# A product of the state-space tables moved behind the next pair of weight chunks, and a memory column moved between two groups of state inputs

## The chip, the core and the metric

The kernel runs on one core of a Trainium2 chip, as one program for the whole inference step. The metric is the device time of one execution in microseconds (us), the median of the runs. The core's engines are called PE (TensorE matmul; PEld is its weight load), DVE (VectorE), ACT (ScalarE), POOL (GpSimd) and SP (SyncE, which here only issues DMAs). Each engine works through its own list of instructions in order; semaphores tie the lists together.

## The reference, cut to what matters

The model is a two-layer decoder trunk on 512 prompt tokens and 8 sample tokens of width 1024, all in float32:

```python
for i in range(2):
    x = x + 0.5 * swiglu(rmsnorm(x), ffn1_w_in[i], ffn1_w_out[i])
    x = x + mixer[i](rmsnorm(x))          # layer 0: S5 state-space block, layer 1: HGRN2
    x = x + cross_attend(rmsnorm(x), mem_k[i], mem_v[i], w_q[i], w_o[i])
    x = x + 0.5 * swiglu(rmsnorm(x), ffn2_w_in[i], ffn2_w_out[i])
y = rmsnorm(x)
mem_k[i], mem_v[i] = split(rmsnorm(mem) @ xattn_w_kv[i])   # 256 memory tokens, 2048 columns
```

The S5 block drives 64 groups of 16 channels, each with a 64-dimensional complex diagonal state: state input B u, a scan over the tokens, output C h + d u. All of these are outputs: the trunk's result, the final states and the memory keys and values.

## The kernel before, in words

**Matmuls.** Every weight matrix is streamed as chunks of 128 columns, two chunks to a pair. A float32 chunk arrives in `raw`, ACT rounds it to a high part `w_hi` (line 1330), DVE subtracts to get a low part `w_lo` (lines 1827 and 1833), and PE multiplies high x high, high x low and low x high into the bank `lin` (lines 3019 and 3024). `ffn1_out0` of layer 0 has four pairs with 11 tiles to a chunk; behind it comes `ffn1_in1`, with 8 tiles to a chunk.

**The tables of the state-space block.** While the first feed-forward block runs, the S5 tables are made. POOL builds eight parts a = 0 to 7 in order; for each one it makes `sFe` and then `sGe` with twelve tensor operations (lines 736 to 738) and counts up `s5_tables` after each of the two (line 1191 for `sGe`). PE then has three groups per part: two transposes F (line 2560) and one product K (line 2567, then line 2570). K of part a waits in PE's list until `s5_tables` says that `sGe` of part a is there:

```python
pe.wait_ge(s5_tables, 2 * a + 2)
```

The function `hook` runs at the end of a pair, on PE, ACT and DVE alike, and calls `prepare(first, end)` for the range of groups that the dictionary `PREP` names for that pair. Before the change, pair a of `ffn1_out0` takes F, F and K of part a for a = 0 to 3; parts 4 to 7 follow in `ffn1_in1`, each after another two pairs. The eight groups in question use the `mis` banks in turn, four of them, and a group waits until ACT has emptied the bank of the fourth group before it. ACT copies F into `sTF` (line 1462) and K into `sKst` (line 1467). `sKst` is one buffer: the copy of part a waits until SP has written part a - 1 to memory (line 946, eight DMAs). SP does that in its own hook, `K_OUT`; for part 2 it comes behind the weight loads of the first pair of `ffn1_in1`, and the loads of the second pair are queued behind it. POOL may build `sGe` of part a only after PE's K of part a - 2.

**The state-space block.** Its order on PE, ACT and SP is the list `S5_ORDER`. PE transposes the normalised tokens (X, line 2717), transposes them again by chunk (U, line 2724) and multiplies them with the tables (FU, line 2732, 16 matmuls to a group). Groups FU 0 to 7 belong to the first half of the states, FU 8 to 15 to the second. DVE scans the first half while FU 8 to 15 run, and the second half after it. Then come the outputs Y and y.

**The memory columns.** Between these groups PE computes the 16 columns of memory keys and values of layer 0 (`kv_step`, matmuls on line 2512, 24 to a column; line 2523 turns the previous column inside the next one). Before the change columns 0, 1 and 2 stand behind FU 15. Column 0 waits for both halves of the normalised memory, `m_hi` and `m_lo`, 1 MB each, which SP loads (line 818) once FU 7 is done, since `m_hi` lies where the first half's tables lay:

```python
if c == 0:
    pe.wait_ge(mem_in[l], 32)
```

On ACT, `kv_step` empties the column (line 1414), splits the weights two columns ahead (line 1403) and copies the turned column out (line 1425).

Of the kernel before, what the change touches and what calls it, by code (L numbers as in the profile page):

```python
# [134 lines left out]
def trunk_kernel(nc, i_, o_):  # L135
# [137 lines left out]
    c = o_hid + 2 * FRONT + 4096  # L273
    pZ = at("pZ", [P, 2, MH, NS, NS], F32, c); c += 2048
    assert c <= o_hid + KD * FRONT
    c = o_lo + 2 * FRONT + 4096
# [9 lines left out]
    c = o_s0  # L286
# [20 lines left out]
    c = o_hid + (FH + KD) * HTILE  # L307
# [6 lines left out]
    c = o_zeros  # L314
# [9 lines left out]
    c = o_s0  # L324
# [18 lines left out]
    c = o_ah + NJ // 2 * (1 + UC) * 4  # L343
# [297 lines left out]
    PREP = {("ffn1_in0", 0, 0): (0, 4), ("ffn1_in0", 0, 2): (4, 9), ("ffn1_in0", 0, 3): (9, 10)}  # L641
    K_OUT = {}
    for a in range(8):
        PREP["ffn1_out0" if a < 4 else "ffn1_in1", 0, a if a < 4 else 2 * a - 7] = (len(made), len(made) + 3)
        K_OUT["ffn1_out0" if a < 2 else "ffn1_in1", 0, a + 2 if a < 2 else a - 2 if a < 4 else 2 * a - 5] = a
        made += [("F", 2 * a, "act"), ("F", 2 * a + 1, "act"), ("K", a, "act")]
    S5P = Groups(made, s5p_fill, s5p_void, banks=4)
    MEM_NORM = {("ffn1_in0", 0, 4 + v // 2, v % 2): v for v in range(3)}
    MEM_SPLIT = {("ffn1_in0", 0, 5 + (v + 1) // 2, (v + 1) % 2): (v // 4, KD // 4 * (v % 4)) for v in range(8)}
# [25 lines left out]
    KV_AFTER = {None: [0, 1, 2], 0: [3, 4], 1: [5, 6], 2: [7, 8], 3: [9, 10], 4: [11, 12], 5: [13], 6: [14], 7: []}  # L675
    HIDDEN = [(0, 0, 6, 1), (0, 6, 7, 1), (1, 0, 3, 1), (0, 7, 8, 1), (1, 3, 6, 2), (1, 6, 8, 2)]
    assert sum(part[3] for part in HIDDEN) == KD
    S5_ORDER = []
    for q, (what, a, _) in enumerate(made):
        S5_ORDER.append(("group", q))  # L680
        if q + 1 == S5G.after("FU"):
            S5_ORDER += [("kv", c) for c in KV_AFTER[None]]
        if what == "Y" and a[1] == 1:
            S5_ORDER += [("kv", c) for c in KV_AFTER[a[0]]]
    S5_ORDER.append(("kv", KV - 1))
# [55 lines left out]
    with block:  # L741
        @block.sync
        def _(sp):
# [179 lines left out]
            def hook(name, layer, i):  # L923
# [8 lines left out]
                if at_ in K_OUT:  # L932
                    a = K_OUT[at_]
                    sp.wait_ge(s5_tables, 2 * a + 2)
                    for e in range(2):
                        sp.dma_start(s5_g[4 * a:4 * a + 4, :, P * e:P * (e + 1)].rearrange("j p n -> p j n"),
                                     sGe[a % 2][:, e, :, 1:, :].rearrange("p j d c -> p j (d c)"))\
                            .then_inc(s5_g_out[a % 2], 16)
                    S5P.emptied_of(sp, "K", a)
                    row = SG * 256  # L940
# [76 lines left out]
        def _(pool):  # L1017
# [11 lines left out]
            pool.nop().then_inc(s5_small, 1)  # L1029
            S5P.all_emptied(pool, S5P.at("m", 3) + 1)  # L1030
            step.link(pool.tensor_tensor(m_acc[:], mT[:, 0, :], mT[:, 0, :], ALU.mult))
# [74 lines left out]
            def s5_discretize():  # L1106
# [3 lines left out]
                pool.wait_ge(mem_squares, 1)  # L1110
                S5P.emptied_of(pool, "par", 0)
                ar, ai, ld = par[:, 0:32], par[:, 32:64], par[:, 64:96]
# [54 lines left out]

                S5P.emptied_of(pool, "c", (1, 1))
                pool.wait_ge(s5p_fill, S5P.at("c", (1, 1)) + 1)
                pool.wait_ge(vec_done, 1)  # L1170
# [8 lines left out]
                for a in range(8):  # L1179
# [7 lines left out]
                    if a >= 2:  # L1187
                        pool.wait_ge(s5p_fill, S5P.at("K", a - 2) + 1)
                        pool.wait_ge(s5_g_out[a % 2], 16 * 2 * (a // 2))
# [1995 lines left out]
```

## Time and profile before

| what | value |
|---|---|
| runs shown | 2360.42, 2360.5 and 2362.08 us, median 2360.5 |
| the profiled execution | 2360.95 us, of which the span from first to last instruction is 2359.2 |
| mean granted clock of TensorE | 0.998 of full speed |
| busy share of the span | PE 99%, PEld 96%, DVE 55%, ACT 37%, POOL 26% |
| the chain that ended last | PE 91%, DVE 4%, POOL 2%, ACT 1%, issue 1%, DMA 1% |

The profile is of one execution. Times in it are microseconds from the first instruction. A busy PE leaves the other engines room; what counts are the few places where PE stands idle or runs at the lower clock.

### The profile page before, as it was taken

How to read it: one execution, taken by the hardware profiler on the slowest of the kernel's cores; microseconds unless marked ns; L12 is line 12 of the kernel's file. 1: busy time of each engine (PE TensorE's matmuls, PEld its weight loads, DVE VectorE, ACT ScalarE, POOL GpSimd, SP SyncE). 2: the span in 40 equal slices, each digit the busy share in tenths (PEclk: the TensorE clock that was granted, in tenths of full speed). 3: DMA queues.
4: the chain of work that ended last, by engine and by line, in shares of the span. 5: the costliest groups of instructions: out<-in, count | busy, mean ns of one | idle time of the engine just before them, and what ended most of it. 6: DMA issues, size and time to landing. Idle time of an engine off the chain costs nothing.

```text
span 2359.2 us, 50146 instructions
## 1 busy us (share of the span) xinstructions
PE 2335.6 (99%) x21043; PEld 2273.7 (96%) x21043; DVE 1295.1 (55%) x1906; ACT 869.1 (37%) x1399; POOL 605.4 (26%) x591
## 2 busy tenths in 40 slices
PE   9999999999999999999999999999999999999999
PEld 8999999889979999999999999999999979999999
DVE  6653643964576443445543344577777666443443
ACT  4432333453233321322433233267775233321323
POOL 3779967431103000004111010432122102000003
PEclk9999999999999999999999999999999999999999
DMA  5456445553563333333543333233332653333332
GB/s 160 130 160 153 122 136 165 175 171 107 161 245 86 98 99 89 98 96 98 159 118 111 100 108 115 83 100 107 104 108 77 214 188 91 97 94 94 98 94 94
DMA packets 483707, 289.19 MB, mean 123 GB/s; under 512 B 22289, under 2 KB 466962, under 8 KB 482514
## 3 DMA queue, kind: packets, MB, share of 16 engines
q1 hardware_dynamic: 477856, 280.66, 40.3%
q0 software_dynamic: 560, 1.84, 0.6%
q10 hardware_dynamic: 5122, 4.25, 0.5%
q8 instruction: 129, 2.11, 0.4%
q14 instruction: 40, 0.33, 0.0%
HBM read 258.86 MB, written 27.85 MB: 122 GB/s over the span
## 4 chain that ended last, share of the span: by engine, by line
PE 91%; DVE 4%; POOL 2%; ACT 1%; issue 1%; DMA 1%; SPq 0%; DVEq 0%; POOLq 0%; ACTq 0%
PE lin L3019 51%; PE lin L3024 25%; PE mis L2512 4%; PE mis L2650 1%; PE mis L2633 1%; POOL sTmp L737 1%; PE lin L2600 1%; PE lin L2762 1%; PE lin L2981 1%; PE lin L2757 1%; POOL sGe L738 0%; PE lin L2650 0%; DVE w_lo L1827 0%; PE mis L2626 0%; POOL sFe L738 0%
## 5 line engine op out<-in xcount | busy, mean ns | idle before, releaser
L1827 DVE TENSOR_TENSOR w_lo<-raw,w_hi 128x1024 fp32r<-128x1024 f32 (+1 forms) x322 | 463.8, 1440 | 294.4 <-ACT w_hi L1330 293.7
L1330 ACT ACTIVATE w_hi<-raw 128x1024 fp32r<-128x1024 f32 (+1 forms) x328 | 365.1, 1113 | 311.3 <-PE lin L3024 257.7
L3019 PE MATMUL lin<-a_rear,w_hi 128*128 128x264 f32 x3552 | 455.6, 279 | 0.0
L3019 PE MATMUL lin<-a_front,w_hi 128*128 128x256 f32 x3552 | 451.6, 279 | 1.1 <-DVE a_rear L1840 0.7
L3019 PEld LDWEIGHTS lin<-a_rear,w_hi 128*128 128x128 f32 x3552 | 432.7, 188 | 0.0
L3019 PEld LDWEIGHTS lin<-a_front,w_hi 128*128 128x128 f32 x3552 | 424.5, 188 | 4.6 <-issue 1.8
L3024 PE MATMUL lin<-a_rear,w_lo 128*128 128x264 f32 x1776 | 245.1, 278 | 0.0
L3024 PE MATMUL lin<-a_front,w_lo 128*128 128x256 f32 x1776 | 240.6, 277 | 0.9 <-DVE w_lo L1827 0.9
L2391 DVE SCALAR_TENSOR_TENSOR xT<-lin,xT 128x520 f32<-128x520 f32 (+1 forms) x87 | 60.8, 699 | 322.9 <-PE lin L3024 322.2
L1063 POOL TENSOR_TENSOR acc<-xT 128x520 f32<-128x520 f32 x8 | 12.2, 1520 | 864.0 <-DVE xT L2391 836.0
L3024 PEld LDWEIGHTS lin<-a_rear,w_lo 128*128 128x128 f32 x1776 | 223.8, 188 | 0.0
L3024 PEld LDWEIGHTS lin<-a_front,w_lo 128*128 128x128 f32 x1776 | 219.6, 188 | 1.6 <-DVE w_lo L1827 1.5
L1741 ACT ACTIVATE f_front<-t 128x256 fp32r<-128x256 f32 (+1 forms) x88 | 36.9, 419 | 398.3 <-DVE t L2372 398.3
L3019 PE MATMUL lin<-f_rear,w_hi 128*128 128x264 f32 x1386 | 179.9, 283 | 0.0
L3019 PEld LDWEIGHTS lin<-f_rear,w_hi 128*128 128x128 f32 x1386 | 172.1, 189 | 0.2
L3019 PE MATMUL lin<-f_front,w_hi 128*128 128x256 f32 x1386 | 170.3, 276 | 0.0
L3019 PEld LDWEIGHTS lin<-f_front,w_hi 128*128 128x128 f32 x1386 | 163.3, 188 | 0.0
L1737 ACT ACTIVATE t<-t 128x520 f32<-128x520 f32 x88 | 56.5, 642 | 270.4 <-DVE t L2366 270.4
L2370 DVE TENSOR_TENSOR t<-lin,rstd 128x520 f32<-128x520 f32 x88 | 61.5, 699 | 161.4 <-PE lin L3024 161.4
L1067 POOL TENSOR_TENSOR sqt<-xT 128x520 f32 (+1 forms) x54 | 81.9, 1517 | 211.0 <-DVE xT L2391 148.8
L3019 PE MATMUL lin<-g_all,w_hi 128*128 128x264 f32 (+1 forms) x1024 | 128.8, 278 | 0.0
L3019 PEld LDWEIGHTS lin<-g_all,w_hi 128*128 128x128 f32 x1024 | 122.7, 188 | 1.1 <-DVE g_all L1967 1.1
(512 smaller groups left out, 3182.7 us busy)
## 6 DMA issues: line engine op xcount, KB each, us to landing
raw<-in_ffn_w_in_dram SPq DMA_DIRECT2D x176, 512.0 KB, 3.9
raw<-in_ffn_w_out_dram SPq DMA_DIRECT2D x64, 704.0 KB, 4.6
kc<-in_cache_mem_k_dram SPq DMA_DIRECT2D x32, 512.0 KB, 6.8
vc<-in_cache_mem_v_dram SPq DMA_DIRECT2D x16, 1024.0 KB, 9.7
raw<-in_hg_w_in_dram SPq DMA_DIRECT2D x32, 512.0 KB, 4.2
raw<-in_xattn_w_kv_dram SPq DMA_DIRECT2D x16, 512.0 KB, 4.4
raw<-in_s_w_glu_dram SPq DMA_DIRECT2D x16, 512.0 KB, 3.9
raw<-in_xattn_w_q_dram SPq DMA_DIRECT2D x16, 512.0 KB, 3.9
```

The lines of the kernel that those rows point to most:

```text
L737: link(eng.tensor_tensor(tmp, pv[1], mv[1 - e], ALU.mult))
L1067: step.link(pool.tensor_tensor(sqt[:], tile(xT, m), tile(xT, m), ALU.mult))
L1330: act.activation(w_hi[:, j, 0:kt, :], raw[:, j, 0:kt, :], ACT.Copy).then_inc(hi_ready, 1)
L1737: act.activation(t2[:], t1[:], ACT.Silu).then_inc(gate_out, 1)
L1741: ins = act.activation(tile(out, i), t3[:, cols], ACT.Copy)
L1827: dve.tensor_tensor(low_weights(n, j), raw[:, j, 0:kt, :], w_hi[:, j, 0:kt, :].bitcast(F32), ALU.subtract).then_inc(lo_ready, 1)
L2370: step.link(dve.tensor_tensor(t4[:], lflat(1), rstd[:], ALU.mult))
L2391: dve.scalar_tensor_tensor(out=tile(xT, m), in0=lflat(j), scalar=scale, in1=tile(xT, m), op0=ALU.mult, op1=ALU.add)\
L2512: ins = pe.matmul(kv_bank(c)[:, 0:NM], w[:, e, k, :], x[:, k, :], start=k == 0 and u == 0, stop=k == KD - 1 and u == 2)
L2600: ins = pe.matmul(lin[32 * h:32 * h + NS, 1, 0, 0:NM], pZ[:, t, h, b, :], vc[layer][V_SLOT[b]][:, t, h * NM:(h + 1) * NM], start=False, st ...
L3019: pe.matmul(lpart(j, half), high[:, k, :], (x_lo if u else x_hi)[half][:, k, :], start=start and u == 0 and k == 0, stop=False)
L3024: ins = pe.matmul(lpart(j, half), low[:, k, :], x_hi[half][:, k, :], start=False, stop=k == kt - 1)
```

## The change

Two edits to the order of work; no instruction is added or taken away.

```diff
@@ -644,6 +644,8 @@
         PREP["ffn1_out0" if a < 4 else "ffn1_in1", 0, a if a < 4 else 2 * a - 7] = (len(made), len(made) + 3)
         K_OUT["ffn1_out0" if a < 2 else "ffn1_in1", 0, a + 2 if a < 2 else a - 2 if a < 4 else 2 * a - 5] = a
         made += [("F", 2 * a, "act"), ("F", 2 * a + 1, "act"), ("K", a, "act")]
+    (late, end), (_, after_late) = PREP["ffn1_out0", 0, 2], PREP["ffn1_out0", 0, 3]
+    PREP["ffn1_out0", 0, 2], PREP["ffn1_out0", 0, 3] = (late, end - 1), (end - 1, after_late)
     S5P = Groups(made, s5p_fill, s5p_void, banks=4)
@@ -678,8 +680,10 @@
     S5_ORDER = []
     for q, (what, a, _) in enumerate(made):
         S5_ORDER.append(("group", q))
+        if (what, a) == ("FU", 11):
+            S5_ORDER += [("kv", c) for c in KV_AFTER[None][:1]]
         if q + 1 == S5G.after("FU"):
-            S5_ORDER += [("kv", c) for c in KV_AFTER[None]]
+            S5_ORDER += [("kv", c) for c in KV_AFTER[None][1:]]
         if what == "Y" and a[1] == 1:
             S5_ORDER += [("kv", c) for c in KV_AFTER[a[0]]]
```

The first edit takes K of part 2 out of the hook of pair 2 of `ffn1_out0` and puts it at the head of the hook of pair 3, which then runs K2, F6, F7, K3. The second puts memory column 0 behind FU 11, ahead of FU 12 to 15; columns 1 and 2 stay behind FU 15. Both hold on PE and on ACT. On SP the list `S5_ORDER` gives the same DMAs in the same order, and `K_OUT` is unchanged.

## Rows read from the trace of the kernel before

**Rows 1.** List of waits of PE: line, releaser, us in total, times, longest
```profile
PE mis L2567 <- POOLq L1191: 2.8, 1, 2.8
PE lin L2732 <- issue: 2.1, 1, 2.1
```
**Rows 2.** Timeline of PE around the products (start, us, instructions, [idle <- releaser])
```profile
177.50 2.89 PE L3019 MATMUL lin<-f_rear,w_hi 128*128 128x264 f32 x22
...
193.04 1.03 PE L2560 MATMUL mis<-ident,sTF 128*128 128x128 f32 x8
196.92 0.64 PE L2567 MATMUL mis<-sGe,bZ 128*32 128x128 f32 x16 [2.84 <-POOLq L1191]
...
197.54 4.47 PE L3019 MATMUL lin<-f_rear,w_hi 128*128 128x264 f32 x22
...
214.53 1.03 PE L2560 MATMUL mis<-ident,sTF 128*128 128x128 f32 x8
215.88 0.64 PE L2567 MATMUL mis<-sGe,bZ 128*32 128x128 f32 x16 [0.31 <-ACT sTF L1462]
...
216.50 1.65 PE L3019 MATMUL lin<-a_front,w_hi 128*128 128x256 f32 x12
```
**Rows 3.** Timeline of POOL: end of parts 2 and 3, one slow operation
```profile
193.87 2.86 POOL L738 TENSOR_TENSOR sGe<-sGe,sTmp 128x576 f32<-128x576 f32 x1
...
208.43 2.69 POOL L738 TENSOR_TENSOR sGe<-sGe,sTmp 128x576 f32<-128x576 f32 x1
...
214.26 1.42 POOL L738 TENSOR_TENSOR sGe<-sGe,sTmp 128x576 f32<-128x576 f32 x1
```
**Rows 4.** Timeline of DVE: the weight splits beside POOL's part 3
```profile
207.70 2.13 DVE L1827 TENSOR_TENSOR w_lo<-raw,w_hi 128x1408 fp32r<-128x1408 f32 x1
209.75 2.05 DVE L1833 TENSOR_TENSOR w_lo<-raw,w_hi 128x640 fp32r<-128x640 f32 x1
...
215.34 0.75 DVE L1833 TENSOR_TENSOR w_lo<-raw,w_hi 128x384 fp32r<-128x384 f32 x1
```
**Rows 5.** Windows: PE, PEld, DVE, ACT, POOL busy, granted clock, DMA share, GB/s
```profile
199.00:200.00 1.00, 1.00 (x6) 1.00 (x6) 0.00 (x0) 0.23 (x1) 0.92 (x2) 0.50 1.08 98
```
**Rows 6.** Timelines of ACT and SP: copy of product 3, stores of product 2
```profile
217.87 0.28 ACT L1467 ACTIVATE sKst<-mis 128x128 f32<-128x128 f32 x1 [1.62 <-DMA s_t<-sKst]
...
211.87 4.16 SPq L946 DMA_DIRECT2D s_t<-sKst  x8
```
**Rows 7.** Timeline of PE in the state-space block, FU 11 to column 1
```profile
431.09 1.28 PE L2732 MATMUL mis<-sU,sTF 128*64 128x80 f32 x32
432.19 0.44 PE L2732 MATMUL lin<-sU,sTF 128*64 128x80 f32 x7
434.69 1.61 PE L2732 MATMUL lin<-sU,sTF 128*64 128x80 f32 x41 [2.05 <-issue]
436.23 1.20 PE L2512 MATMUL mis<-m_hi,w_hi 128*128 128x256 f32 x8
...
439.07 1.07 PE L2512 MATMUL mis<-m_hi,w_hi 128*128 128x256 f32 x8
```
**Rows 8.** Issue of the second memory half on SP, and DMA view (KB, us to landing)
```profile
427.05 0.43 SPq L818 DMA_DIRECT2D m_lo<-mem_split  x1
...
m_lo<-mem_split SPq DMA_DIRECT2D x1, 1024.0 KB, 8.0
```
**Rows 9.** DMA queues in 432.1 to 433.2; windows while PE stood
```profile
q8 instruction: 1, 0.02, 5.0%
...
433.00:434.00 1.00, 0.00 (x0) 0.00 (x0) 0.96 (x2) 0.00 (x0) 0.00 (x0) 1.00 0.35 131
434.00:435.00 1.00, 0.31 (x9) 0.31 (x10) 1.00 (x1) 0.00 (x0) 0.00 (x0) 1.00 0.02 8
```
**Rows 10.** ACT's table load behind FU 15; DVE's scan of the second half
```profile
436.80 1.28 ACT L1616 ACT_TABLE_LOAD   x1
...
459.77 3.08 DVE L2114 TENSOR_TENSOR rot_tmp<-rotC,sFH 128x1024 f32<-128x1024 f32 x1 [0.24 <-DVE sFH L2130]
```

## The prediction, made before the changed kernel was run

> **What bounds the kernel now.** I read the page's first part, then PE's list of waits, then the timelines around the two places that the change touches. PE is busy 99% of the span and the chain of waits is 91% PE, so only time in which PE stands, or runs at the lower clock, can be won or lost. In the list of waits [rows 1] two entries belong to the change: line 2567, the table product K, waited 2.8 us for POOL once, and line 2732, a state input FU, stood 2.1 us once for "issue", that is for nothing the profile shows.
>
> The first stall is K of part 2: F4 and F5 end at 194.07 and K2 starts at 196.92 [rows 2], 0.19 after POOL ended `sGe` of part 2 (193.87 + 2.86 = 196.73) [rows 3]. It has a tail. The next 22 matmuls took 4.47 us where the same 22 took 2.89 one pair earlier [rows 2], and the granted clock in that stretch is 0.50, the 1.2 GHz level [rows 5]; that is 1.58 us lost. PE had stood 2.84 us just before the clock fell.
>
> The second stall lies inside FU 13, after 7 of its matmuls [rows 7], where no semaphore is waited for. One packet of instructions, 0.02 MB, moved in the same stretch [rows 9], so I take it for the fetch of PE's own code. The clock stayed at 1.00 through it [rows 9].
>
> **Edit 1: K2 one pair later.** No instruction is added; 24 small matmuls of K2 (0.62 us, from 215.88 to 216.50) [rows 2] move. Without the stall pair 3 starts at 194.07. Pair 2, with the same shapes, needed 193.04 - 177.50 = 15.54 us [rows 2], so pair 3 ends at 209.6, K2 at 210.2, F6 and F7 (1.03) at 211.2. Then PE is at K3, which needs `sGe` of part 3.
>
> That table is ready at 214.26 + 1.42 = 215.68 [rows 3]. In the profile K3 starts at 215.88, 0.20 after it, the same lag as K2's. So although the row names ACT's copy [rows 2], it was POOL that released K3. POOL's part 3 asks only for K1, so nothing in the change starts it earlier. K3 starts at 215.88 again and PE stands from 211.2 to 215.88, 4.7 us. Gone are 2.84 + 0.31 + 1.58 = 4.7 us; come are 4.7 us. The stall isn't removed, it is gathered at K3, and what is late next is the same engine, POOL, with the next table.
>
> Two things are left over. First the clock: it now falls behind K3 instead of behind K2, and the first chunk of `ffn1_in1`, from 216.50 [rows 2], pays for it. The bounds are 0 (as in the 2.05 us stall) and 1.58; the new stall is longer than the one that lowered the clock, so I stand near the upper end, at 1.3, since part of the low stretch can fall into the stall itself. Second, POOL's own pace: DVE's weight splits follow PE's chunks. Two of them already lie beside part 3, and an operation of line 738 took 2.69 us beside a split against 1.42 for the last [rows 3, 4]. The third, 384 columns at 215.34 [rows 4], touches only part 3's end; 4.9 us earlier it falls inside. Bounds: -1.27 (the splits land so that POOL loses no operation to them) and +1.27 (one more operation as slow as that one); I take +0.4, about half of the split's 0.75 us.
>
> The Trainium skill, SBUF — State Buffer, section Who interferes with whom, says that a VectorE instruction with two SBUF inputs and a GpSimd instruction that reads SBUF exclude each other for the whole instruction. The 2.69 against 1.42 agrees in kind. By that rule alone the third split could hold POOL for its whole 0.75 us, and edit 1 would come out 0.35 us later than my sum.
>
> The other queues that the step passes: ACT copies K3 only when K2's eight stores have landed. SP comes to them some 4.7 us earlier and then waits for K2's copy at about 210.5; the stores take 4.16 us to issue, and the last landed about 1.8 us after (216.03 to 217.87) [rows 6], so K3's copy runs at about 216.6, when K3 is just done, against 217.87 before. The weight loads behind the stores on SP leave at 214.7 instead of 216.0. This costs nothing as long as that 1.3 us of slack holds; were it gone, the second chunk of `ffn1_in1` would start late by what is missing. POOL's part 4 needs K2, done by 210.2, before POOL is through with part 3. Edit 1: 0 + 1.3 + 0.4 = +1.7 us, bounds -1.3 and +2.9.
>
> **Edit 2: memory column 0 behind FU 11.** FU 11 and 12 are the 32 matmuls from 431.09, 1.28 us [rows 7], so FU 11 ends at 431.7. The column waits for both halves of the memory. The second half is issued at 427.05 and lands 8.0 us later, at 435.05 [rows 8]; before, the column started at 436.23 and never felt it. FU 7, which frees the place for the load, comes at the same moment as before. So PE stands from 431.7 to about 435.15. The column takes 439.07 - 436.23 = 2.84 us, and FU 12 to 15, queued behind it, 64 matmuls at 41 in 1.61 us [rows 7], 2.4 us without the last one's tail. Column 1 starts at 435.15 + 2.84 + 2.4 = 440.4 instead of 439.07: +1.3 us. The 2.05 us of fetch are hidden under the new wait, which is longer. Bounds: -2.05 if the memory is there at 431.7, +1.3 as worked out.
>
> The clock again: PE stands 3.4 us, more than the 2.84 that lowered it and more than the 2.05 that didn't. Between 0 and 1.58 I take the middle, 0.8.
>
> What waits for FU 12 to 15 costs nothing. DVE scans the second half only from 459.77 [rows 10]; ACT's table load of 1.28 [rows 10] now runs beside column 1, which is as long as column 0, so the copies of column 0 are out before column 2 asks for the bank. Without that cover PE would wait some tenths of a us, at most the 1.28. Edit 2: +1.3 + 0.8 = +2.1 us.
>
> **Sum.** The profiled execution took 2360.95 us, 1.75 of it outside its span of 2359.2, and lies 0.45 above the median. 2360.95 + 1.7 + 2.1 = 2364.75; on the median's scale 2364.3.
>
> **Rivals.** (1) *Faster: the stalls simply go.* If `sGe` of part 3 were ready when PE comes to K3 and the memory when PE leaves FU 11, 4.7 + 2.05 = 6.8 us are won: 2353.7. It decides at 211.2, so POOL would have to be 4.5 us quicker in one part; its one visible loss to DVE there is 1.27 us. 5%.
>
> (2) *No change.* Of the memory's second half little is still moving after 434.0: 131 GB/s in the microsecond before, 8 in the one after [rows 9]. If its landing is told at 434.0, the column starts 1.05 us sooner and edit 2 is +0.25; with no drop of the clock and POOL 0.4 quicker instead of slower, the total is about -0.2: 2360.3. The Trainium skill, DMA: Bandwidth & Descriptors, section Queues, rings and completion order, says that a DMA's semaphore step lands only after all earlier writes of that DMA engine, whatever their queue; by it one instruction packet on one engine can hold back the whole landing, and a packet at another moment would give this rival its 1.05 us. Nothing here shows that the packet moves, since the list of PE is unchanged up to FU 11. 17%.
>
> (3) *Slower: the clock falls in full behind both new stalls.* Each costs 1.58, with edit 1's POOL delay at its bound of 1.27 and edit 2's 1.3: 1.58 + 1.27 + 1.58 + 1.3 = 5.7 us, 2366.2. For it speaks that both stalls are longer than the one that lowered the clock; against it that a low stretch may lie partly in the stall. It decides where both drops cost over 1 us. 23%.
>
> **How the numbers follow.** 55% for the forecast, whose own range is 2361.5 to 2366.0 (no clock drop at all, to both nearly whole). About 0.2%, 4.7 us, is what a measurement of this kernel tells from no change. Slower by more: rival 3 and 0.05 of the forecast's upper end, 0.28. Faster by more: rival 1 and a little, 0.06. Within: 0.66. The range for 8 in 10 takes in most of rivals 2 and 3: 2360.2 to 2367.0.
>
> **What would show it.** Right: PE's list of waits has K for POOL once, near 211 to 216, of 4 to 5 us, and no stall at 194; the pair behind K2's old place runs at full clock, the chunk behind K3 partly at 0.50; line 2512's first matmul waits for the DMA of `m_lo` some 3 us, and no "issue" is left on line 2732. Wrong: K3 starting before 215, or column 0 starting at 432 without a wait.

## The result and the profile after

| | median of the runs | lowest to highest |
|---|---|---|
| before | 2360.67 us (12 runs) | 2357.33 to 2363.77 |
| after | 2364.58 us (12 runs) | 2362.94 to 2371.98 |

The ratio of after to before is 1.0019, with a 95% interval of 1.0011 to 1.0026: 2.6 to 6.1 us longer, the middle of it 4.5. The medians differ by 3.9 us. The forecast was 3.8 us longer, 2364.3. That is a small loss, and it sits just under the 0.2% that the prediction named as what can be told, though the interval excludes no change. In the experiments, one execution of 13356.0 us (three products later) and one of 4732.36 us (the same with the halves apart) count as slow: the ratios leave them out, the medians given don't.

The profiled execution after took 2362.94 us, its span 2361.2, PE busy in 99% of it. In the list of waits of PE (columns as in [rows 1]) one entry stands in the place of each of the two of before. Beside these only the wait for the first rows of the input is over 1.3 us.

```profile
PE mis L2571 <- POOLq L1195: 5.1, 1, 5.1
PE mis L2516 <- issue: 3.3, 1, 3.3
```

Line numbers are four higher now: 2571 is the product K (2567 before), 2516 the memory column (2512), 2736 the state inputs FU (2732), 2564 the transposes F, 1195 POOL's count for `sGe`.

**The products.** PE's timeline, against [rows 2]:

```profile
193.36 1.03 PE L2564 MATMUL mis<-ident,sTF 128*128 128x128 f32 x8
194.15 2.86 PE L3023 MATMUL lin<-f_rear,w_hi 128*128 128x264 f32 x22
...
209.60 0.64 PE L2571 MATMUL mis<-sGe,bZ 128*32 128x128 f32 x16
...
210.22 1.09 PE L2564 MATMUL mis<-ident,sTF 128*128 128x128 f32 x8
216.39 1.08 PE L2571 MATMUL mis<-sGe,bZ 128*32 128x128 f32 x16 [5.07 <-POOLq L1195]
...
217.48 2.49 PE L3023 MATMUL lin<-a_front,w_hi 128*128 128x256 f32 x12
```

The reader is to see four things. Nothing stands at 194 any more, and the 22 matmuls behind F4 and F5 take 2.86 us, full speed, in place of 4.47. K2 runs at 209.60 without a wait. K3 stands 5.07 us, for POOL. And K3 itself takes 1.08 us in place of 0.64, the 12 matmuls behind it 2.49 in place of 1.65: the clock fell behind the new stall. The windows say so (columns as in [rows 5]):

```profile
216.00:217.00 1.00, 0.61 (x13) 0.64 (x17) 0.00 (x0) 0.00 (x0) 0.35 (x2) 0.50 0.95 280
...
218.00:219.00 1.00, 1.00 (x7) 1.00 (x6) 0.14 (x1) 0.83 (x1) 0.92 (x2) 0.50 0.91 116
219.00:220.00 1.00, 1.00 (x9) 1.00 (x9) 1.00 (x1) 0.00 (x0) 0.94 (x1) 0.85 0.61 76
```

POOL's timeline, against [rows 3], has the end of part 2, the operation beside the third split, and the end of part 3:

```profile
194.33 2.75 POOL L742 TENSOR_TENSOR sGe<-sGe,sTmp 128x576 f32<-128x576 f32 x1
...
210.53 1.61 POOL L742 TENSOR_TENSOR sGe<-sGe,sTmp 128x576 f32<-128x576 f32 x1
...
214.80 1.40 POOL L742 TENSOR_TENSOR sGe<-sGe,sTmp 128x576 f32<-128x576 f32 x1
```

From the end of part 2 (197.08) to the end of part 3 (216.20) are 19.12 us; before it was 215.68 - 196.73 = 18.95. POOL's pace is the same to 0.17 us, and K3 again starts 0.19 after POOL. The third split of DVE now lies inside part 3, as expected, and it took 0.55 us (0.75 in [rows 4]):

```profile
210.33 0.55 DVE L1837 TENSOR_TENSOR w_lo<-raw,w_hi 128x384 fp32r<-128x384 f32 x1
```

**The column.** PE's timeline, against [rows 7]:

```profile
431.70 0.72 PE L2736 MATMUL mis<-sU,sTF 128*64 128x80 f32 x16
435.72 1.17 PE L2516 MATMUL mis<-m_hi,w_hi 128*128 128x256 f32 x8 [3.30 <-issue]
...
438.62 0.77 PE L2736 MATMUL mis<-sU,sTF 128*64 128x80 f32 x16
439.23 1.83 PE L2736 MATMUL lin<-sU,sTF 128*64 128x80 f32 x48
440.99 1.22 PE L2516 MATMUL mis<-m_hi,w_hi 128*128 128x256 f32 x8
```

FU 13 runs through: its 48 matmuls with FU 14 and 15 take 1.83 us, and the 2.05 us of "issue" inside it are gone. In their place the column's first matmul stands 3.30 us, and PE is at full clock through it:

```profile
434.00:435.00 1.00, 0.00 (x0) 0.00 (x0) 0.96 (x2) 0.00 (x0) 0.00 (x0) 1.00 0.04 16
```

The DMA view puts the landing of the second half at 8.0 us after its issue (427.66), as before. The column's first matmul starts 0.1 us behind that landing:

```profile
m_lo<-mem_split SPq DMA_DIRECT2D x1, 1024.0 KB, 8.0
```

**By stretches.** Runs start up to 4 us apart, by the first rows of the input. So I measure from the first matmul of F4 on, between the starts of the same matmuls of each profile; only the last column goes to the end of the last matmul.

| profile | F4 to K4 | first to last X | last X to column 1 | F4 to the last matmul's end |
|---|---|---|---|---|
| before | 46.74 | 15.06 | 17.28 | 2161.87 |
| after | 48.25 | 13.72 | 18.59 | 2163.56 |
| edit 1 alone | 49.69 | 13.40 | 17.51 | 2163.57 |
| edit 2 alone | 46.76 | 15.05 | 18.95 | 2163.98 |
| before, code shifted | 46.76 | 13.40 | 15.01 | 2158.17 |

The second column is a trap. Among the transposes X of the state-space block the clock falls in some profiles and not in others: it is 0.50 from 418 to 420 in before, and 1.00 in after. That is worth 1.3 to 1.7 us. Six of the thirteen profiles have it (before, edit 2 alone, two products later, halves apart, wait filled, changed and shifted), and no edit is in these six alone. How often it falls in the runs that were not profiled isn't known. This profile of before has it and this one of after hasn't, so the two profiles differ by only 1.7 us from F4 on, while the medians differ by 3.9.

### The profile page after: what moved, and what is told of

Same layout as the page of the kernel before. It is cut to its first block, busy times and chain, and to the rows that moved or that the text cites. A ratio compares the mean times of both kernels' runs of the same rounds, so it can differ in the third digit from the quotient of the medians.

```text
span 2361.2 us, 50146 instructions
## 1 busy us (share of the span) xinstructions
PE 2333.1 (99%) x21043; PEld 2271.4 (96%) x21043; DVE 1295.2 (55%) x1906; ACT 868.7 (37%) x1399; POOL 606.2 (26%) x591
## 4 chain that ended last, share of the span: by engine, by line
PE 77%; DVE 3%; ACT 1%; issue 1%; DVEq 0%; ACTq 0%
PE lin L3023 43%; PE lin L3028 21%; PE mis L2516 4%; PE mis L2654 1%; PE mis L2637 1%; PE lin L2604 1%; PE lin L2766 1%; PE lin L2761 1%; PE lin L2654 0%; PE mis L2630 0%; PE mis L2816 0%; PE mis L2804 0%; PE lin L2902 0%; PE mis L2527 0%; PE lin L2736 0%
```

## The experiments

Each was timed beside the kernel before on the same chip. Ratios are to that kernel.

**1. Edit 1 alone, edit 2 alone.** Each kernel has one hunk of the change.

> The first edit alone: K2 behind pair 3, memory columns as before. Theory (POOL's table 3 releases K3): no stall at K2, one of 4.5 to 5.1 us at K3, which starts about 216 as before; TensorE at 1.2 GHz right behind it for part of the next chunk. Time +1.0 to +2.2 us against before. Rival (the stall at K2 is simply gone): K3 starts near 211, time -4.7 us.

> The second edit alone: memory column 0 behind FU 11, products as before. Theory (column 0 waits for the landing of the second memory half): column 0 starts 0.1 us after that landing, about 3.3 us after FU 11's end, column 1 starts 1.3 us later than before. Time +1.3 us, up to +2.9 where the clock falls in the wait. Rival (the fetch stall is saved and nothing takes its place): -2.05 us.

Edit 1 alone: 2362.39 us against 2360.19, ratio 1.0011 (1.0002 to 1.0020). Edit 2 alone: 2362.32 us, ratio 1.0008 (0.9999 to 1.0017). The middles are 2.6 and 1.9 us and add up to the 4.5 of both, so neither edit is a gain that the other spoils. The interval of edit 2 just takes in no change. PE's timeline with edit 1 alone:

```profile
215.77 1.08 PE L2569 MATMUL mis<-sGe,bZ 128*32 128x128 f32 x16 [5.07 <-POOLq L1193]
...
216.86 2.93 PE L3021 MATMUL lin<-a_front,w_hi 128*128 128x256 f32 x12
219.59 2.66 PE L3021 MATMUL lin<-a_rear,w_hi 128*128 128x264 f32 x12
```

The stall is the same, 5.07 us, but here the second dozen is at half speed as well (2.66; 1.62 at full): the clock stayed low for 6.8 us, against 3.4 in the profile of after. So the price behind one stall varies. By these matmuls against those at full speed it is 0.44 + 0.84 = 1.3 us in after and 0.44 + 1.28 + 1.04 = 2.8 us here.

With edit 2 alone the old stalls of K are both there (2.84, and 0.35 before K3), and this profile names POOL for K3's short wait, where [rows 2] named ACT's copy. The column starts at 433.65 after 3.57 us of "issue", at full clock, again 0.1 us behind the landing of `m_lo`.

**2. Two products later.** K3 is moved as well, to the hook of the first pair of `ffn1_in1`, so that POOL has time (the cut is against edit 1; column 0 stays where it was before).

```diff
-    PREP["ffn1_out0", 0, 2], PREP["ffn1_out0", 0, 3] = (late, end - 1), (end - 1, after_late)
+    PREP["ffn1_out0", 0, 2], PREP["ffn1_out0", 0, 3] = (late, end - 1), (end - 1, after_late - 1)
+    PREP["ffn1_in1", 0, 0] = (after_late - 1, after_late)
```

> The first edit, and K3 too taken one pair later, behind the first pair of ffn1_in1; memory columns as before. Theory (POOL paces the products, and is 4 us ahead one pair later): no wait of PE for POOL at K2 or K3, no drop of the clock there; time -4.7 us against before (2.84 + 0.31 + 1.58). Rival (the gain is given back at a later product, K4 or K5, or through ACT's copy of K3): a new wait for POOL or ACT there and a time within 1 us of before.

2358.88 us, ratio 0.9987 (0.9978 to 0.9997). K2 and K3 run without a wait; the next product, K4, waits:

```profile
234.94 0.64 PE L2570 MATMUL mis<-sGe,bZ 128*32 128x128 f32 x16 [2.14 <-POOLq L1194]
```

From F4 to K4 it is 44.19 us in place of 46.74. The stall moves one product on again, from K3 to K4, but it is shorter there, 2.14 in place of 5.07 us, and no drop of the clock followed it. So the rival was right that the wait turns up again at K4; it gave back only part of the gain.

**3. Three products later.** K2, K3 and K4 all one pair later; F4 to F9 stay.

> K2, K3 and K4 each one pair later (K3 behind the first and K4 behind the third pair of ffn1_in1); memory columns as before. With K2 and K3 later the wait came back at K4, 2.1 us. Theory (POOL paces the products; every part costs it some 19.5 us, two pairs of ffn1_in1 some 23): no wait for POOL at any of the eight products, no drop of the clock there, time -4.7 us against before, 2 us less than with K2 and K3 alone. Rival (the wait goes on to K5): a wait of 1 to 2 us at K5, time as with K2 and K3 alone.

2355.20 us against 2360.71, ratio 0.9981 (0.9970 to 0.9991): 4.5 us faster by the ratio's middle. No wait for POOL is left on any K, and the view of cores shows a clock that never fell:

```profile
core 0: 2351.1 us, clock 1.000
```

This is the version that edit 1 was one third of. It shows that the product is paced by POOL and that the clock's fall at the products goes with the stall, since taking the stall away took both. The thirteen profiles agree: the clock fell beside a K that had stood 2.8 us or more in all seven that have one, and beside no K in the other six. (The drop among the X is missing from this profile too, so not all of its gain on the profile of before is the products'.)

**4. The wait filled.** Edit 1, with 36 transposes of the identity into K3's bank ahead of its wait (K3 overwrites it).

```diff
+                        if a == 3:
+                            for _ in range(36):
+                                pe.transpose(bank[:, 0:P], ident[:], ident[:])
```

> The first edit alone, with 36 extra transposes of the identity into K3's own bank ahead of K3's wait (about 4.2 us of PE; K3 overwrites them). Theory (the stall itself costs what K2's did; the 1.0 to 1.6 us on top is the clock that falls in it): K3 starts when it does with the first edit alone, 0.2 us after POOL's table 3, the clock stays at full speed behind it, and the time is 1.3 us less than with the first edit alone, 0 to +0.5 us against before. Rival (the clock has no part in it): time as with the first edit alone, +2 us.

```profile
212.46 4.09 PE L2567 MATMUL mis<-ident 128*128 128x128 f32 x36
217.65 0.65 PE L2572 MATMUL mis<-sGe,bZ 128*32 128x128 f32 x16 [1.09 <-POOLq L1193]
...
218.27 1.65 PE L3024 MATMUL lin<-a_front,w_hi 128*128 128x256 f32 x12
```

K3 is held by POOL as before (POOL ends part 3 at 217.55), so the wait in time is the same, but K3 takes 0.65 and the dozen behind it 1.65: full clock. 2358.38 us, ratio 0.9989 (0.9980 to 0.9998); by the ratios, 1.0011 and 0.9989, 5 us below edit 1 alone, by the medians 4. That is more than the 2.8 us that the clock took in the profile of edit 1. In the profile the rest sits elsewhere: the "issue" stall in FU 13 is gone, last X to column 1 takes 15.06 us. Edit 1 doesn't touch that place. What the fill had done to it was to push every later instruction of PE 72 places down its list (36 weight loads, 36 matmuls). Experiment 6 takes that up.

**5. The halves of the memory apart.** Edit 2, where column 0 multiplies by `m_hi` first (high and low weights) and waits for `m_lo` by itself, on a semaphore of its own.

```diff
-                pe.wait_ge(mem_in[l], 32)
+                pe.wait_ge(mem_in[l], 16)
...
+                    if c == 0 and x is m_lo[l]:
+                        pe.wait_ge(mem_loaded, 16 * (2 + l))
```

> The second edit alone, with a semaphore for each half of the memory: column 0 multiplies the first half with the high and the low weights (16 matmuls) and only then waits for the second half. Theory (the landing of the second half holds the column): the 16 matmuls run right behind FU 11, the last 8 start 0.1 us after the second half's landing, and column 1 starts 0.6 us earlier than before, 1.9 earlier than with the second edit alone. Time -0.6 us against before. Rival (PE stands for its own code or for something else in front of column 0): the first matmul starts as late as with the second edit alone, time as that one.

2360.42 us, ratio 0.9995 (0.9986 to 1.0004): what edit 2 had cost is gone, nothing more that can be told. Column 1 starts 17.02 us behind the last X, 1.9 earlier than with edit 2 alone and 0.3 earlier than before (0.6 expected).

```profile
430.66 1.10 PE L2519 MATMUL mis<-m_hi,w_lo 128*128 128x256 f32 x8
433.00 1.22 PE L2519 MATMUL mis<-m_lo,w_hi 128*128 128x256 f32 x8 [1.24 <-DMA m_lo<-mem_split]
```

Two groups of matmuls now run inside the old wait, and the third waits 1.24 us for the DMA of `m_lo`, this time by name. It settles what "issue" on line 2516 was: the landing of the second half, not a fetch of code.

With the three products of experiment 3 as well:

> The three products later and the memory column behind FU 11 with a semaphore for each half of the memory. Theory (the two places don't touch each other): the sum of both, -4.7 and -0.3, so -5.0 us against before; PE's list of waits names neither K nor FU, and the column's last third waits about 1.2 us for the DMA of m_lo. Rival (POOL or the DMAs give part of it back): -2 to -3 us.

2355.92 us against 2360.71, ratio 0.9977 (0.9966 to 0.9988). Against the three products alone it is no difference that can be told. The column's last third waited 0.8 us for `m_lo`, not 1.2.

**6. The code shifted.** The kernel before, with the 36 transposes at the very start of PE's list, where PE waits for the first rows of the input.

```diff
             pe.wait_ge(consts_done, 4)
+            for _ in range(36):
+                pe.transpose(mis[:, 0, 0:P], ident[:], ident[:])
```

> The kernel before with 36 transpositions of the identity put at the very start of PE's list, where PE waits for the first rows of the input anyway (their results are overwritten by the first rows). Nothing else changes, so the stall of K2 (2.84 us) and its tail stay. Theory: the 2.05 us of 'issue' inside FU 13 belong to a place in PE's list of instructions, so shifting the list by as many instructions as in the run before (the wait filled) takes it away there: column 1 to the glu step takes about 15.1 us instead of 17.3 and the time is 2 us shorter, some 2358.5. Rival A: the 2.05 us come from the load of the memory that runs at the time; then the stall stays in FU 13 and the time is the one of before, 2360.5. Rival B: the stall only turns up elsewhere, in other matmuls that nothing hides: FU 13 without it, the time unchanged.

(The stretch that it calls "column 1 to the glu step" is the one from the last X to column 1.)

2357.56 us, ratio 0.9992 (0.9983 to 1.0002): 2.9 us lower by the medians, but the interval just takes in no change. The profile is plain: FU 13 runs through, and the column follows at once, without a wait.

```profile
430.03 1.83 PE L2734 MATMUL lin<-sU,sTF 128*64 128x80 f32 x48
431.83 1.16 PE L2514 MATMUL mis<-m_hi,w_hi 128*128 128x256 f32 x8
```

So the 2.05 us go with a place in PE's list, not with the load of the memory by itself, which was under way here as well. (That PE waits there for its own code is the likely reading, not shown; whether the load makes such a fetch slow is not separated by this.) The four profiles that have the stall (before, edit 1 alone, two and three products later) have it before the same matmul of FU 13. Edit 2 moves FU 13 down the list by the 48 instructions of column 0; the old place is then the first weight load of FU 12, which in after follows the column without such a stall. The time alone wouldn't prove the point, since the clock fell less as well: the mean granted clock is 0.9989 over these runs and 0.9981 over those of before beside them. And the load itself came out shorter, by the DMA view:

```profile
m_lo<-mem_split SPq DMA_DIRECT2D x1, 1024.0 KB, 6.9
```

It landed 6.9 us after its issue, not 8.0. In the eight profiles whose code isn't shifted a packet of instructions started 5.1 to 5.6 us after the issue and the landing took 8.0 to 8.4; in the five that are shifted (the filled one, this one and the three below) the packet came 6.3 to 6.5 us after the issue, and the landing took 6.8 to 7.0. The packets show how. In before the packet of instructions took 0.88 us and ended 6.03 us after the load's issue. At 6.02 a packet of the load began, the first of three in a row of which the last ended at 7.5, and the landing followed; everything else of the load was over by 6.5. So one DMA engine came to its last three packets only behind the instructions. (Which engine a packet is on isn't recorded; in all eight profiles a packet of the load starts as the instructions end.) Between 6.5 and 7.6 us after the issue the load's queue still has data in before, first line, and a 4-byte packet alone in the shifted kernel, second line:

```profile
q1 hardware_dynamic: 3, 0.02, 3.6%
q1 hardware_dynamic: 1, 0.00, 0.1%
```

The sentence on the Trainium skill in rival 2 of the prediction (DMA: Bandwidth & Descriptors, Queues, rings and completion order) agrees in what follows from it: one packet on one engine held back the whole landing, by 1.1 us. But here the load's own data came late on that engine, which is more than the order in which a semaphore step may land.

Experiment 4 can now be read: against this kernel the filled edit 1 is 2358.38 to 2357.56 us, and 46.89 to 46.76 us from F4 to K4. With the clock held up, edit 1 costs nothing that can be told: its one stall of 5.1 us at full clock is about as long as the two of before (3.2 us) with the low clock behind K2 (1.6 us).

The changed kernel, shifted in the same way:

> The changed kernel with the 36 transpositions at the start of PE's list. Theory: the packet of instructions that moved during the load of the memory's second half made it land 8.0 us after its issue; with the packet at another moment it lands after 6.9 us, as in the two shifted runs before. Column 0 then waits some 2.2 us instead of 3.3, and K3 waits about 5.1 us as in the changed kernel: some 1.05 us off 2364.6, 2363.5, still 5 to 6 us above the shifted kernel before (2357.6), because its fetch stall is no longer there to be hidden. Rival: the landing of 8.0 us belongs to the load itself, the column waits 3.3 us again: 2364.5.

```profile
PE mis L2573 <- POOLq L1195: 5.1, 1, 5.1
PE mis L2518 <- issue: 2.2, 1, 2.2
```

The column waits 2.2 us where it waited 3.3, and last X to column 1 takes 17.55 us, 1.04 less than in after: the theory's step is there. The expected time is not, it is the rival's: 2364.54 us against 2361.37, ratio 1.0012 (1.0003 to 1.0021). In this profile the clock stayed low for 6.8 us behind K3 and fell among the X too, and 1.4 us more went to waits behind the columns (the matmuls of the gated unit, which end the block, begin 90.84 us after column 1; 89.43 in after). A gain of 1 us can't be told here from the clock's comings and goings. Against the shifted kernel before, edit 2 costs 17.55 - 15.01 = 2.5 us in its stretch, not 1.3: there is no fetch for its wait to hide.

**7. The best of both.** The three products later, shifted: first with edit 2 and the memory's halves apart, then without edit 2.

> The kernel with all three products later and the memory's halves apart (2355.9), with the same 36 transpositions at the start of PE's list. Theory: there the fetch of code was already hidden under the wait for the memory's second half, so the shift can win only what a packet of instructions held back that landing, at most 0.85 us: 2355.0 to 2356. Rival: the shift brings a fetch to a place where nothing hides it: 1.5 to 2 us longer, 2357.5 to 2358.

> Three products one pair later, the column where it was before, and the 36 transpositions at the start of PE's list. Theory: no wait of K, no stall in FU 13, no wait for the memory: 1.5 us off 2355.2, some 2353.7, the shortest of all. Rival: the time is bound by what comes before, or the shift brings a fetch elsewhere: 2355 or more.

2356.76 us, ratio 0.9985 (0.9976 to 0.9994), and 2355.52 us, ratio 0.9977 (0.9968 to 0.9986). By the medians neither is under the 2355.20 of the three products alone; by the ratios the second is 0.9 us better, which the noise covers. The first came out above its 2355.0 to 2356, without reaching its rival's; my 2353.7 for the second was not reached, and the rival's 2355 or more held. In the last one the stall of FU 13 is gone as the theory had it (last X to column 1 takes 15.13 us; 17.51 unshifted). What it won was lost to the next in line, by its list of waits and its timeline:

```profile
PE lin L2764 <- DMA sTabG<-s_g: 1.0, 2, 0.8
...
236.39 2.10 PE L3026 MATMUL lin<-a_front,w_hi 128*128 128x256 f32 x16 [1.11 <-ACT w_hi L1335]
```

F4 to K4 takes 54.88 us against 53.48 (a weight chunk came late from memory, so ACT's split did), and a table's load was waited for at 507. Whether the late chunk is the shift's doing or that one execution's stays open; the other shifted kernel with three products has 54.79 there, its unshifted twin of experiment 5 53.03.

## Why the prediction was right, point by point

**Edit 1, the stall gathered at K3: right.** 5.07 us were measured for 4.7. F6 and F7 end at 211.3 (211.2 predicted) and K3 starts 0.5 later than the 215.88 predicted, of which 0.32 is the profile's later start and 0.17 POOL's. That POOL and not ACT released K3 was read from a lag of 0.20 us against the row's own word; edit 2 alone names POOL for it, and three products later takes it away.

**Edit 1, the clock: right in kind, mis-sized upward.** I put 1.3 us, with 1.58 as the upper bound, from the one drop in before. It measured 1.3 in after, and 2.8 with edit 1 alone, as the low stretch was 3.4 us once and 6.8 another time. So the upper bound was not one: a single row bounds nothing that varies.

**Edit 1, POOL: mis-sized.** +0.4 was predicted, +0.17 was measured. The third split came, but it took 0.55 us and lay only partly beside one operation, which took 1.61 us against 1.40 for the same operation alone. The rule in the prediction on VectorE and GpSimd (the Trainium skill, SBUF — State Buffer, Who interferes with whom) would have held POOL for the 0.35 us that the two have in common; the trace shows 0.2. The prediction also counted one slow operation in part 3 of before where there are two, the second beside the second split (first line: 1.69 us, where its like took 1.22). In after both long splits come 5 us earlier, at 202.69 and 204.78, and slow two other operations by as much, 1.27 and 0.47 us (second and third line: 1.11 and 1.28 undisturbed). So POOL's pace held because the price moved along with the splits:

```profile
211.19 1.69 POOL L736 TENSOR_TENSOR sGe<-pw,cT 128x576 f32<-128x576 f32 x1
...
203.46 2.38 POOL L741 TENSOR_TENSOR sTmp<-pw,bBar 128x512 f32<-128x512 f32 x1
205.91 1.75 POOL L742 TENSOR_TENSOR sFe<-sFe,sTmp 128x512 f32<-128x512 f32 x1
```

**Edit 1, the other queues: right, with other times.** SP's stores of K2 left at 210.68 and the weight loads behind them at 214.38 (214.7 predicted). ACT's copy of K3 ran at 217.61, not 216.6, since K3 was itself late and slow; it cost nothing.

**Edit 2, the wait: right.** Column 1 starts 18.59 us behind the last X in place of 17.28: +1.31 for +1.3. The landing, the 2.84 us of the column (2.90) and the old stall hidden under the wait are all as worked out. Wrong was what the list would call it: it says "issue". A wait on a DMA's landing can stand under that word, and only the run with a semaphore for each half showed it.

**Edit 2, the clock: wrong.** I put 0.8 us, half of a drop, for a stall of 3.4. None of the profiles with the column moved shows a drop there (waits of 3.30, 3.57 and 2.18 us), while 2.84 us in before did lower it. Length of the stall alone doesn't decide; what does was not found.

**The sum.** 1.7 + 2.1 = 3.8 was predicted. By stretches it is 1.5 + 1.3 = 2.8 in after's profile; by the medians 3.9, by the ratio's middle 4.5. In after's profile the sum is 1 us short, by the column's 0.8 that didn't come and POOL's 0.2; the medians come out at the forecast because other executions lost more elsewhere, so the closeness is in part luck. The clock behind K3 makes the difference most likely, as it cost more in the profile of edit 1 alone. The granted clocks of the runs agree: their mean is 0.9971 over the twelve of after, with 0.995 in the two slowest (2370.21 and 2371.98 us), 0.9975 with edit 1 alone, and 0.9982 both with edit 2 alone and over the 96 runs of before in the experiments. So what the clock takes comes with edit 1 and not with edit 2; where in a run it fell, a mean doesn't say. A term that I didn't have is the drop among the X, 1.3 to 1.7 us, which is in the profile of before and which I took for part of the kernel.

**The rivals.** The stalls didn't simply go: POOL was not quicker at part 3 in any run (18.95 us at the least, as in before). What rival 2 needed, a landing 1 us sooner, exists, experiment 6 has it: 1.1 us of the landing go with a packet whose moment moves with the code. In the changed kernel the packet was where it had been, as its list is unchanged up to FU 11. Rival 3's full drop behind K3 came about with edit 1 alone (2.8 us), the one behind the column did not.

## What to carry to other kernels

A consumer that is paced by a producer gains nothing when one of its steps is moved: the stall goes to the next step and comes out longer in one piece, and here the low clock behind it made a loss of it (2.6 us by the ratio). Move all the steps that the producer is late for: two gave 3.1 us by the ratio, three 4.5.

Before a step is put into a gap, ask what it waits for itself. The column needed a load that ended 3.2 us later; two thirds of its matmuls needed only the half that was already there.

Where a stall has no releaser in the profile and an instruction packet moves in it, shift the code before explaining it by the data: 36 transposes at the start showed that the stall goes with the place in the list.

## What the runs showed of the hardware that was not expected

- PE stood 2.05 us (1.5 in two other kernels) in the middle of a group of small matmuls, before the same matmul each time, most likely for its own code. It goes with the position in the list: shifted by 72 instructions, it was gone.
- One packet of instructions, 0.02 MB, that moved inside a 1 MB load came ahead of the load's last three or four packets on one engine, and the landing came later by 1 us or more (8.0 to 8.4 us against 6.8 to 7.0). With edit 2 the landing is on PE's path, so the fetch of code then delays PE's data.
- A stall of 5.07 us lowered the clock to 0.50 for 3.4 us in one profile and 6.8 us in two others. Stalls of 3.30 and 3.57 us among the small matmuls of the state-space block left it at 1.00.
- 36 transposes of the identity in a wait kept the clock up behind it and cost nothing that can be told.
- Two weight splits of DVE cost POOL 1.27 and 0.47 us in before and in after, beside different operations each time.
